# Attention of a decoder layer in float32: values' parts in one operand, scores over half the rows, keys projected before part of the queries, WO's high parts on two engines

## The chip, the cores and the metric

One core of one Trainium2 chip runs the kernel. The metric is the device time of one execution in microseconds (us); lower is better. Engines are named as in the profile: PE is TensorE (its weight loads PEld), DVE is VectorE, ACT is ScalarE, POOL is GpSimd, SP starts the DMAs.

## The reference

One layer over 1024 rows of width 1024, all in float32. The part that the change touches is the token mixer, sliding-window attention with 16 query heads and 4 key/value heads of 64:

```
u   = rmsnorm(x, mix_g)
qkv = u @ wqkv                     # 1024 x 1536
q   = rmsnorm(q heads, gq);  k = rmsnorm(k heads, gk)
s   = q . k / 8 - slope[h] * dist  # per 128-row block, over its own and the previous block
p   = softmax of s within 0 <= dist < 128, with one learned sink per head in the denominator
h   = x + (p @ v) @ wo
```

After it come a squared-ReLU MLP of width 4096 and a gated embedding, which the change leaves alone.

## The kernel before

Products of float32 numbers are made from two parts of each operand: HI, the value rounded to the type float32r, and LO, what is left. A product then takes three passes over TensorE (`PASSES`: HI-HI, HI-LO, LO-HI). For an operand that another engine makes, ACT copies the HI part out of PSUM or a raw buffer and DVE subtracts to make the LO part.

The attention stage walks over 8 blocks of 128 rows (`body(n)`), each in 4 groups (`j`), one group for each key/value head and its 4 query heads. Every engine has its own list of instructions with this order written out by hand, and the engines meet at semaphores; an engine never goes past a wait. In the parts' names, `k` is the projection of keys and values (512 columns), `q0` and `q8` those of query heads 0 to 7 and 8 to 15.

TensorE's list in a block (`body`, L1999): scores of the group (L1947), then what belongs to the group, then `weigh_values` of two groups ago (L1973), then `turn_probs` of the last group (L1963, transposes of the probabilities). Group 0 has the last 6 matmuls of q8 ahead of its scores and `turn_x` (L1891, the next block's x). Group 1 has the next block's q0 projection with `turn_q` of q8 (L1935) between its fifth and sixth k-tile; group 2 has the projection of `k`; group 3 `turn_q` of q0, 18 matmuls of q8 and `turn_k` (L1924).

Scores: q's HI part stands in one half of the 128 rows of `qT` and its LO part in the other, while k stands in both halves of `kT`, as HI and as LO. So a full-row matmul with k's HI and one with k's LO give all four products of a head: 8 matmuls of 256 columns a group. Values: `vz` keeps each head's values between zeros, so that a matmul of 128 weight columns and 256 moving columns puts two heads of a pair on the upper or the lower 64 output rows: 3 passes, 2 sides and 2 halves of keys make 12 matmuls of 256 columns, all summed in one bank. ACT copies that bank out in one instruction (`attention_out`, L949).

DVE in a group: `add_bias` (L1366) merges the two halves of keys with two predicated copies (L1374), adds the bias and takes the maximum for four heads (L1387) and makes `nmax` (L1392). ACT's `exps` (L931) follow, then DVE's `invert` and `scale_probs` (L1401), PE's `turn_probs`, ACT's `pT_hi_part` (L942), DVE's `pT_lo_part` (L1408), POOL's `mask_probs` (L757).

The heads' normalisation of each part is `part_squares` on ACT (L876), `head_sums` on DVE (L1305), `head_norm` on POOL (L688: the variance L691 and the power L693), `head_scale` on DVE (L1311), `turn_q` or `turn_k` on PE, and then HI on ACT (L914, L923) and LO on DVE (L1333, L1340). All three parts put their squares into the one buffer `kn`, so each waits for the one before it.

The last block (`last_part`, L961 and L1413) has no next block to project. In its place TensorE starts the projection by WO for row blocks 0 and 1 (`project_out`, L2033), for which ACT makes WO's eight HI units (`wo_hi_unit`, L857) and DVE the eight LO units (`wo_lo_unit`, L1489). SP and its DMAs are the same in both kernels.

## Time and profile before

| what | value |
|---|---|
| median of 3 runs | 1109.57 us (1107.19 to 1109.82) |
| the profiled execution's own time | 1107.26 us |
| its span, first to last instruction | 1105.5 us |
| PE busy | 98% of the span |
| DVE, ACT, POOL busy | 66%, 39%, 13% |
| granted PE clock | 1.0 of 2.4 GHz |

Busy time is summed over an engine's instructions. Consecutive matmuls overlap in the profile, since each is drawn with its way through the array; the pace of a stretch is read from the chain of waits, which gives the pieces one after another. The chain is followed back from the last instruction: at each step to what released it, or to the instruction before it on its engine. In a timeline the number in brackets is the engine's idle time before the instruction, and what ended it.

### The profile page before, as it was taken

To read this page: it belongs to the slowest core of one execution; us is meant where nothing else is said; L and a number is where in the kernel's file an instruction comes from. 1 tells how busy PE (TensorE), PEld (TensorE's weight loads), DVE (VectorE), ACT (ScalarE), POOL (GpSimd) and SP (SyncE) were. 2 spreads that over 40 slices of the span, in tenths; PEclk is the share of its full clock that TensorE was granted. 3 is DMA by queue.
4 is the path that set the end of the run, shared out by engine and by line. 5 is a ranking of instruction groups with operands and counts; after the bars stand their busy time and mean duration, and the time that the engine had idled before them with its cause. 6 is when DMAs were issued, how large, how long until landed. Compare 5 with 4: busy or idle time off the path is not lost.

```text
span 1105.5 us, 14894 instructions
## 1 busy us (share of the span) xinstructions
PE 1084.9 (98%) x5272; PEld 910.3 (82%) x5272; DVE 732.2 (66%) x1130; ACT 429.8 (39%) x776; POOL 148.4 (13%) x272
## 2 busy tenths in 40 slices
PE   7899999998999999999999999999999999999998
PEld 5788888887888888888888888888888888888886
DVE  6677777778454599776667667598777862664222
ACT  7455655566322234323232244453333331333100
POOL 6554444444100000000000000000000000110000
PEclk9999999999999999999999999999999999999999
DMA  7000000040242325254434056998988862112211
GB/s 267 20 20 20 19 19 0 38 184 26 92 138 76 114 73 209 118 191 153 153 132 190 39 191 218 390 411 293 299 285 289 288 227 76 39 39 59 95 39 39
DMA packets 61361, 153.88 MB, mean 139 GB/s; under 512 B 4720, under 2 KB 5752, under 8 KB 61304
## 3 DMA queue, kind: packets, MB, share of 16 engines
q1 hardware_dynamic: 61280, 153.12, 39.0%
q8 instruction: 35, 0.57, 0.2%
q14 instruction: 22, 0.18, 0.1%
q10 hardware_dynamic: 24, 0.01, 0.0%
HBM read 119.03 MB, written 34.08 MB: 138 GB/s over the span
## 4 chain that ended last, share of the span: by engine, by line
PE 90%; DVE 5%; issue 2%; ACT 1%; POOL 1%; ACTq 0%; DVEq 0%; POOLq 0%
PE pair L2204 24%; PE pair L2184 21%; PE pair L1919 10%; PE pair L2056 8%; PE pair L2247 8%; PE pair L2224 4%; PE pair L1990 4%; PE pair L2142 3%; PE pair L1958 2%; PE pair L2260 2%; PE pair L2112 1%; PE pair L1969 1%; PE pair L1943 1%; PE pair L1901 0%; DVE RES L1722 0%
## 5 line engine op out<-in xcount | busy, mean ns | idle before, releaser
L2204 PE MATMUL pair<-uT 128*128 128x512 f32 x1176 | 266.7, 389 | 0.0
L2204 PEld LDWEIGHTS pair<-uT 128*128 128x128 f32 x1176 | 220.7, 188 | 45.8
L1193 ACT ACTIVATE uT<-wo_raw 128x1024 fp32r<-128x1024 f32 x63 | 64.4, 1054 | 104.9 <-PE pair L2204 90.4
L1919 PE MATMUL pair<-WA,xT 128*128 128x512 f32 x384 | 95.9, 398 | 5.3 <-DVE WA L1292 3.8
L1735 DVE TENSOR_TENSOR uT<-wo_raw,uT 128x1024 fp32r<-128x1024 f32 x63 | 74.9, 1221 | 38.8 <-ACT uT L1193 38.7
L675 POOL TENSOR_SCALAR row_var<-row_ssq 128x1 f32<-128x1 f32 x16 | 3.0, 191 | 700.3 <-ACT hn L1092 700.3
L2056 PE MATMUL pair<-WA,oT 128*128 128x512 f32 x384 | 90.3, 392 | 2.6 <-DVE WA L1491 2.1
L1919 PEld LDWEIGHTS pair<-WA,xT 128*128 128x128 f32 x384 | 69.6, 188 | 22.4 <-issue 6.8
L2056 PEld LDWEIGHTS pair<-WA,oT 128*128 128x128 f32 x384 | 71.2, 188 | 17.5 <-issue 3.1
L2184 PE MATMUL pair<-WA,WB 128*128 128x512 f32 x336 | 78.2, 389 | 0.4 <-ACT xr L1168 0.4
L2184 PEld LDWEIGHTS pair<-WA,WB 128*128 128x128 f32 x336 | 63.0, 188 | 13.8 <-DVE WB L1669 0.8
L938 ACT ACTIVATE probs<-probs,nmax 128x129 f32<-128x129 f32 x128 | 50.0, 393 | 42.8 <-DVE nmax L1392 42.6
L2184 PE MATMUL pair<-uT,WB 128*128 128x512 f32 x240 | 56.1, 389 | 0.0
L2184 PEld LDWEIGHTS pair<-uT,WB 128*128 128x128 f32 x240 | 45.0, 188 | 9.6 <-issue 0.3
L1990 PE MATMUL pair<-pT,vz 128*128 128x256 f32 x384 | 52.1, 285 | 0.5 <-DVE pT L1410 0.5
L1990 PEld LDWEIGHTS pair<-pT,vz 128*128 128x128 f32 x384 | 49.1, 190 | 2.1 <-DVE pT L1410 0.7
L1867 DVE TENSOR_TENSOR act_buf<-pair,act_buf 128x512 f32<-128x512 f32 x16 | 11.0, 690 | 55.3 <-PE pair L2260 55.3
L1919 PE MATMUL pair<-WB,xT 128*128 128x512 f32 x192 | 45.3, 391 | 1.7 <-DVE WB L1292 1.7
L1826 DVE TENSOR_TENSOR RES<-RES,pair 128x512 f32<-128x512 f32 x48 | 30.8, 682 | 22.2 <-PE pair L2204 22.2
L2224 PE MATMUL pair<-WA 128*128 128x512 f32 x192 | 45.4, 393 | 0.0
L2247 PE MATMUL pair<-WB,uT 128*128 128x512 f32 x192 | 45.2, 391 | 0.0
L2247 PE MATMUL pair<-WA,uT 128*128 128x512 f32 x192 | 44.8, 389 | 0.0
(203 smaller groups left out, 1876.1 us busy)
## 6 DMA issues: line engine op xcount, KB each, us to landing
wo_raw<-in_m_w SPq DMA_DIRECT2D x53, 512.0 KB, 6.3
wo_raw<-hid_kept SPq DMA_DIRECT2D x36, 512.0 KB, 4.6
hid_kept<-RES SPq DMA_DIRECT2D x28, 512.0 KB, 2.6
emb<-in_m_w SPq DMA_DIRECT2D x20, 512.0 KB, 6.2
RES<-in_m_w SPq DMA_DIRECT2D x8, 1024.0 KB, 6.9
uT_f<-in_m_w SPq DMA_DIRECT2D x6, 1024.0 KB, 6.5
act_buf<-hid_kept SPq DMA_DIRECT2D x11, 512.0 KB, 4.4
hn<-in_m_w SPq DMA_DIRECT2D x11, 512.0 KB, 5.7
```

The lines of the kernel that those rows point to most:

```text
L938: ex = nc.scalar.activation(row, row, ACT.Exp, bias=nmax[:, i, r:r + 1], accum_out=denom[:, i, r:r + 1])
L1193: nc.scalar.activation(operand(t, which, HI), unit(t, which), ACT.Copy).then_inc(op_hi, 1)
L1735: nc.vector.tensor_tensor(operand(t, which, LO), unit(t, which), operand(t, which, HI).bitcast(F32), ALU.subtract).then_inc(op_ready, 1)
L1826: nc.vector.tensor_tensor(RES[:, b, cols], RES[:, b, cols], bank[:], op).then_inc(posted, 1)
L1919: mm = nc.tensor.matmul(proj_bank[X][:], xT[:, s, kt, :], w[:, m, kt, at:at + BANK], start=(kt == 0 and i == 0), stop=(kt == KT - 1 and i ...
L1990: mm = nc.tensor.matmul(pv_bank[:, 0:2 * P], vz[:, kt, s, at:at + 2 * HD], pT[:, m, kt, odd * 2 * P:(odd + 1) * 2 * P], start=(done == 0), ...
L2056: mm = nc.tensor.matmul(out_bank(b, odd, c)[:], oT[:, hf, s, k % 4 * P:(k % 4 + 1) * P], wo_s[:, m, k, c * BANK:(c + 1) * BANK], start=(k ...
L2142: mm = nc.tensor.matmul(ps[i % 4][:], w1_s[:, s, kt, m * P:(m + 1) * P], uT[:, r, kt, th * BANK:(th + 1) * BANK], start=(kt == 0 and q == ...
L2184: mm = nc.tensor.matmul(chain[:, m, :], a_slot[q % 4][:, s, k, m * P:(m + 1) * P], right(i)(r)[:, k, :], start=(opens and k == 0 and n == ...
L2204: mm = nc.tensor.matmul(ps[4 * (j % 2) + m][:], operand(t, 0, s)[:, k, m * P:(m + 1) * P], operand(t, 1, r)[:, k, :], start=(g == 0 and k ...
L2224: mm = nc.tensor.matmul(ps[4 + a % 4][:], hid[:, s, k, b * P:(b + 1) * P], w2_s[:, r, k, c * BANK:(c + 1) * BANK], start=(k == 0 and q == ...
L2247: mm = nc.tensor.matmul(ps[4 + s % 2][:], uT[:, u, kt, b * P:(b + 1) * P], w[:, m, kt, :], start=(kt == 0 and q == 0), stop=(kt == KT - 1 ...
```

## The change

- **Values.** `vz` holds HI and LO of a head side by side as one operand of 128 weight columns. Four matmuls of 512 columns a group give both parts' products: HI values on output rows 0 to 63, LO values on 64 to 127. ACT copies the bank out in four pieces of 64 rows and 256 columns, and DVE adds the LO half in `add_lows`, three groups later in its list. The LO-LO product, left out before, is in. TensorE waits with `pv_copied` for the bank; the rest waits with `attended`.
- **Scores.** `qT` holds two heads on its two halves of rows, HI and LO as separate tiles. Three passes, each over 64 rows, make 12 matmuls of 256 columns a group; neighbouring ones use opposite halves of the rows and different banks. Both gains of the norms are put on the keys. The two predicated copies become one of 512 columns (`merge_scores`).
- **Order.** Each part has its own buffer for squares. TensorE projects three k-tiles of `k` in group 1, the other five and q0's last three in group 2, and turns q0 at the end of group 3 behind `turn_k`. The heads' sums, norms and scales move in ACT's, DVE's and POOL's lists accordingly; on ACT `pT_hi_part` now stands ahead of `attention_out`.
- **WO.** HI units 4 to 7 are made by POOL, 0 to 3 by ACT, and in the last block DVE's LO units stand at other places.

```diff
 Q8_HEAD, Q8_TAIL = range(0, 6), range(6, 8)
+Q0_HEAD, Q0_TAIL = range(0, 5), range(5, 8)
+K_HEAD, K_TAIL = range(0, 3), range(3, 8)
...
+vz = sb("vz", [P, 2, KV, 2, HD], F32R, in_a)
+low_out = sb("low_out", [P, 2, 2 * P], F32, in_a)
...
 pT = sb("pT", [P, 2, 2, BANK], F32R, in_a)
 probs = sb("probs", [P, 2, G, P + 2], F32, in_a)
...
+score_keys = pair[1][:].rearrange("p b (h a n) -> p (b h) a n", h=2, a=2)
 pT_bank = (ps[4], ps[5])
...
+    def wo_hi_unit(k):
+        pool.wait_ge(projected["q8"], NB)
+        pool.wait_ge(wb_in[k], 16)
+        copy(wo_s[:, HI, k, :], wo_raw[:, k, :]).then_inc(wo_hi_pool, 1)
     def place_sinks(n, j):
...
@@ -779,19 +783,25 @@
             x_norm(n + 1)
         place_sinks(n, 2)
         dv_hi_part(n)
-        if not last:
-            head_norm("q0", n + 1)
         mask_probs(4 * n)
-        if not last:
+        if last:
+            wo_hi_unit(4)
+        else:
             keep_v(n)
         place_sinks(n, 3)
         if not last:
             head_norm("k", n + 1)
         mask_probs(4 * n + 1)
-        if not last:
+        if last:
+            wo_hi_unit(5)
+        else:
             shift_k(n + 1)
             place_sinks(n + 1, 0)
+            head_norm("q0", n + 1)
         mask_probs(4 * n + 2)
+        if last:
+            wo_hi_unit(6)
+            wo_hi_unit(7)
     pool.wait_ge(consts_in, 16)
     place_sinks(0, 0)
...
         if j == 3:
+            head_norm("q0", 1)
             mask_probs(2)
     place_sinks(1, 0)
...
+        wait(act, turned[X], b)
         cols = NH[X] * HD
-        nc.scalar.activation(kn[:, 0:cols], proj_bank[X][:, 0:cols], ACT.Square).then_inc(squared[X], 1)
+        nc.scalar.activation(heads[X][:, 0:cols], proj_bank[X][:, 0:cols], ACT.Square).then_inc(squared[X], 1)
...
-    def q_hi_part(X, b, odd):
+                             ACT.Copy, scale=g_both[:]).then_inc(T_hi["k"], 1)
+    def q_hi_part(X, b):
         act.wait_ge(turned[X], b + 1)
...
-        wait(act, scores_ready, 8 * b + (-4 if X == "q0" else 0))
-        rows = q_rows(odd, HI)
-        nc.scalar.activation(qT[rows, q_heads(X, odd), :], turn_bank[X][rows, :].rearrange("p (a n) -> p a n", a=G),
-                             ACT.Copy, scale=gq_s[rows, :]).then_inc(T_hi[X], 1)
+        wait(act, scores_ready, 4 * b + (-2 if X == "q0" else 0))
+        nc.scalar.activation(qT[:, HI, q_pairs(X), :], turn_bank[X].rearrange("p (a n) -> p a n", a=G),
+                             ACT.Copy).then_inc(T_hi[X], 1)
...
         t, i = 4 * n + j, j % 2
...
         act.wait_ge(w_split, U_W1)
         act.wait_ge(pv_done, t + 1)
+        wait(act, attended, t - 1)
         dst = RES[:].rearrange("p b n -> p (b n)")[:, bass.ds(n * D + j * 2 * P, 2 * P)]
-        nc.scalar.activation(dst, pv_bank[:, 0:2 * P], ACT.Copy).then_inc(attended, 1)
+        nc.scalar.activation(dst[0:HD, :], pv_bank[0:HD, 0:2 * P], ACT.Copy)
+        nc.scalar.activation(low_out[HD:P, j % 2, :], pv_bank[HD:P, 2 * P:4 * P], ACT.Copy)
+        nc.scalar.activation(low_out[0:HD, j % 2, :], pv_bank[HD:P, 0:2 * P], ACT.Copy)
+        nc.scalar.activation(dst[HD:P, :], pv_bank[0:HD, 2 * P:4 * P], ACT.Copy).then_inc(pv_copied, 1)
...
@@ -962,25 +962,18 @@
         t = 4 * n + j
         if j == 0:
             wo_hi_unit(0)
-            wo_hi_unit(1)
-            exps(n, j)
-            attention_out(n - 1, 2)
-            pT_hi_part(t - 1, (j - 1) % 2)
-            q_hi_part("q8", n, 0)
-            q_hi_part("q8", n, 1)
-            wo_hi_unit(2)
+        if j == 1:
+            q_hi_part("q8", n)
+        exps(n, j)
+        if j < 2:
+            wo_hi_unit(j + 1)
+        pT_hi_part(t - 1, (j - 1) % 2)
+        attention_out(*before(n, j, 2))
+        if j == 1:
+            v_hi_part(n)
             wo_hi_unit(3)
-            return
-        attention_out(*before(n, j, 2))
         if j == 2:
             oT_hi_half(1, 0)
-        pT_hi_part(t - 1, (j - 1) % 2)
-        if j == 1:
-            v_hi_part(n)
-        exps(n, j)
-        wo_hi_unit(j + 3)
-        if j == 3:
-            wo_hi_unit(7)
...
@@ -991,27 +984,25 @@
                 if not last:
                     xT_hi_half(n + 1, 0)
                     xT_hi_half(n + 1, 1)
-            if j == 3 and not last:
-                q_hi_part("q0", n + 1, 0)
-                q_hi_part("q0", n + 1, 1)
             if last:
                 last_part(n, j)
                 continue
             if j == 1:
-                q_hi_part("q8", n, 0)
-                q_hi_part("q8", n, 1)
+                q_hi_part("q8", n)
+            if j == 2:
+                part_squares("k", n + 1)
+            if j == 3:
+                part_squares("q0", n + 1)
             exps(n, j)
-            if j == 1 and not last:
-                part_squares("q0", n + 1)
-            if j == 2 and not last:
-                part_squares("k", n + 1)
+            if j == 2:
                 stage_v(n + 1)
-            if j == 3 and not last:
+            if j == 3:
                 k_hi_part(n + 1)
+                q_hi_part("q0", n + 1)
+            if not (first and j < 1):
+                pT_hi_part(t - 1, (j - 1) % 2)
             if not (first and j < 2):
                 attention_out(*before(n, j, 2))
-            if not (first and j < 1):
-                pT_hi_part(t - 1, (j - 1) % 2)
             if j == 1:
                 v_hi_part(n)
             if j == 0 and not last:
...
     body(NB - 2)
     body(NB - 1, last=True)
-    attention_out(NB - 1, GROUPS - 2)
     pT_hi_part(NB * GROUPS - 1, 1)
     oT_hi_half(1, 1)
+    attention_out(NB - 1, GROUPS - 2)
     oT_hi_half(2, 0)
     attention_out(NB - 1, GROUPS - 1)
...
+    def q_lo_part(X, b):
+        dve.wait_ge(T_hi[X], b + 1)
+        nc.vector.tensor_tensor(qT[:, LO, q_pairs(X), :], turn_bank[X].rearrange("p (a n) -> p a n", a=G),
+                                qT[:, HI, q_pairs(X), :].bitcast(F32), ALU.subtract).then_inc(T_ready[X], 1)
...
+    def add_lows(n, j):
+        dve.wait_ge(pv_copied, 4 * n + (j + 1))
+        dst = RES[:].rearrange("p b n -> p (b n)")[:, bass.ds(n * D + j * 2 * P, 2 * P)]
+        nc.vector.tensor_tensor(dst, dst, low_out[:, j % 2, :], ALU.add).then_inc(attended, 1)
...
         nc.vector.tensor_tensor(vprev[:], vprev[:], vnext[:], ALU.subtract).then_inc(v_diffed, 1)
     def v_lo_part(b):
-        def values(slot, s):
-            return vz[:, slot, s, HD:(2 * KV + 1) * HD].rearrange("p (v a d) -> p v a d", v=KV, a=2)[:, :, 0, :]
         dve.wait_ge(v_hi, b + 1)
-        nc.vector.tensor_tensor(values(1, LO), vnext[:].rearrange("p (v d) -> p v d", v=KV),
-                                values(1, HI).bitcast(F32), ALU.subtract).then_inc(v_ready, 1)
...
+    def merge_scores(n, j, first):
+        t = 4 * n + j
...
-            stand(dve, scores_ready, 2 * t + (1 + half_bank))
-            nc.vector.copy_predicated(score_keys[half_bank][:, :, 0, :],
-                                      current[:].bitcast(U32).unsqueeze(1).to_broadcast([P, 2, P]),
-                                      score_keys[half_bank][:, :, 1, :]).then_inc(wrapped, 1)
+        stand(dve, scores_ready, t + 1)
+        nc.vector.copy_predicated(score_keys[:, :, 0, :],
+                                  current[:].bitcast(U32).unsqueeze(1).to_broadcast([P, G, P]),
+                                  score_keys[:, :, 1, :]).then_inc(wrapped, 1)
...
-            if r % 2 == 0:
-                stand(dve, wrapped, 2 * t + (1 + r // 2))
+                stand(dve, wrapped, t + 1)
             nc.vector.tensor_tensor_reduce(
-                probs[:, i, r, 0:P], score_keys[r // 2][:, r % 2, 0, :],
+                probs[:, i, r, 0:P], score_keys[:, pos(r), 0, :],
                 bias[:, G * j + r, :], 1.0, 0.0, ALU.add, ALU.max, rmax[:, i, r:r + 1]).then_inc(biased, 1)
...
     def last_part(n, j):
         t = 4 * n + j
+        merge_scores(n, j, False)
+        add_lows(*before(n, j, 3))
+        add_bias(n, j, False)
         if j == 0:
             head_sums("q8", n)
-            add_bias(n, j, False)
-            wo_lo_unit(0)
+        wo_lo_unit((0, 2, 4, 5)[j])
+        invert(n, j)
+        scale_probs(n, j)
+        if j == 0:
             head_scale("q8", n)
+        if j == 1:
+            q_lo_part("q8", n)
+        pT_lo_part(t - 1, (j - 1) % 2)
+        if j == 0:
+            v_diff(n)
             wo_lo_unit(1)
-            pT_lo_part(t - 1, (j - 1) % 2)
-            v_diff(n)
         if j == 1:
-            q_lo_part("q8", n, 0)
-            q_lo_part("q8", n, 1)
-            add_bias(n, j, False)
-            pT_lo_part(t - 1, (j - 1) % 2)
             v_lo_part(n)
-            wo_lo_unit(2)
             wo_lo_unit(3)
         if j == 2:
-            add_bias(n, j, False)
             oT_lo_half(1, 0)
-            pT_lo_part(t - 1, (j - 1) % 2)
-            wo_lo_unit(4)
-        if j == 3:
-            add_bias(n, j, False)
-            pT_lo_part(t - 1, (j - 1) % 2)
-            wo_lo_unit(5)
-        invert(n, j)
-        scale_probs(n, j)
         if j == 3:
             wo_lo_unit(6)
             wo_lo_unit(7)
...
+            merge_scores(n, j, first)
+            if not (first and j < 3):
+                add_lows(*before(n, j, 3))
             add_bias(n, j, first)
             if j == 0:
-                if not last:
-                    xT_lo_half(n + 1, 0)
-                    xT_lo_half(n + 1, 1)
-                head_scale("q8", n)
+                xT_lo_half(n + 1, 0)
+                xT_lo_half(n + 1, 1)
+                head_sums("q8", n)
             if j == 1:
-                q_lo_part("q8", n, 0)
-                q_lo_part("q8", n, 1)
+                q_lo_part("q8", n)
+                v_diff(n)
             if j == 2:
                 if isinstance(n, int) and n == NB - 2:
                     oT_lo_half(0, 0)
                     oT_lo_half(0, 1)
-                if not last:
-                    head_sums("k", n + 1)
-                    head_scale("q0", n + 1)
-                    head_scale("k", n + 1)
-            if j == 3 and not last:
-                q_lo_part("q0", n + 1, 0)
-                q_lo_part("q0", n + 1, 1)
+                head_sums("k", n + 1)
+            if j == 3:
+                head_sums("q0", n + 1)
             invert(n, j)
-            if j == 1 and not last:
-                head_sums("q0", n + 1)
+            if j == 2:
+                head_scale("k", n + 1)
             scale_probs(n, j)
-            if j == 3 and not last:
+            if j == 3:
+                head_scale("q0", n + 1)
                 k_lo_part(n + 1)
+                q_lo_part("q0", n + 1)
             if not (first and j < 1):
                 pT_lo_part(t - 1, (j - 1) % 2)
             if j == 0:
-                v_diff(n)
+                head_scale("q8", n)
             if j == 1:
                 v_lo_part(n)
     flat = RES[:].rearrange("p b n -> p (b n)")
     def wo_lo_unit(k):
-        dve.wait_ge(wo_hi, k + 1)
+        if k < 4:
+            dve.wait_ge(wo_hi, k + 1)
+        else:
...
     nc.vector.tensor_scalar(columns[:, KT:KT + 2], ps[5][:, 0:2], 1.0, None, ALU.mult).then_inc(mix_ready, 1)
     dve.wait_ge(mix_ready, 2)
-    nc.vector.tensor_scalar(gq_s[:], gq_col, HD ** -0.5, None, ALU.mult).then_inc(mix_ready, 1)
+    nc.vector.scalar_tensor_tensor(out=g_both[:], in0=gq_col, scalar=HD ** -0.5, in1=gk_col, op0=ALU.mult,
+                                   op1=ALU.mult).then_inc(mix_ready, 1)
     lo_unit(1, "kv", 1)
...
     oT_lo_half(1, 1)
+    add_lows(NB - 1, 1)
+    add_lows(NB - 1, 2)
...
     add_attention(0, False)
+    add_lows(NB - 1, 3)
...
...
         wait(pe, biased, 4 * t)
-        for r in range(G):
-            dst = score_bank[r // 2][:, (r % 2) * 2 * P:(r % 2 + 1) * 2 * P]
-            for m in (HI, LO):
-                mm = nc.tensor.matmul(dst, qT[:, G * j + r, :], kT[:, m, j, :, :].rearrange("p a n -> p (a n)"),
-                                      start=(m == HI), stop=(m == LO))
-            if r % 2 == 1:
-                mm.then_inc(scores_ready, 1)
+        for a in range(2):
+            for i, (s, m) in enumerate(PASSES):
+                for odd in range(2):
+                    rows = slice(odd * HD, (odd + 1) * HD)
+                    mm = nc.tensor.matmul(score_bank[odd][:, a * 2 * P:(a + 1) * 2 * P],
+                                          qT[rows, s, G // 2 * j + a, :],
+                                          kT[rows, m, j, :, :].rearrange("p a n -> p (a n)"),
+                                          start=(i == 0), stop=(i == 2))
+        mm.then_inc(scores_ready, 1)
...
         for kt in (1, 0):
             if kt == 0:
                 pe.wait_ge(pT_masked, 2 * t + 2)
                 pe.wait_ge(v_ready, 2 * n + 2)
-            for s, m in PASSES:
-                for odd in range(2):
-                    at = 2 * HD * j + (0 if odd else HD)
-                    mm = nc.tensor.matmul(pv_bank[:, 0:2 * P], vz[:, kt, s, at:at + 2 * HD],
-                                          pT[:, m, kt, odd * 2 * P:(odd + 1) * 2 * P],
-                                          start=(done == 0), stop=(done == 11))
-                    done += 1
+            for m in (HI, LO):
+                mm = nc.tensor.matmul(pv_bank[:], vz[:, kt, j, :, :].rearrange("p s d -> p (s d)"),
+                                      pT[:, m, kt, :], start=(done == 0), stop=(done == 3))
+                done += 1
         mm.then_inc(pv_done, 1)
...
+                    project("q0", n + 1, kts=Q0_HEAD)
                 turn_q("q8", n, after_x=not last)
                 if not last:
-                    project("q0", n + 1, kts=range(5, KT))
-            if j == 2:
-                if not last:
-                    project("k", n + 1)
+                    project("k", n + 1, kts=K_HEAD)
+            if j == 2 and not last:
+                project("k", n + 1, kts=K_TAIL)
+                project("q0", n + 1, kts=Q0_TAIL)
             if j == 3 and not last:
-                turn_q("q0", n + 1)
                 project("q8", n + 1, kts=range(KT) if isinstance(n, int) and n == NB - 2 else Q8_HEAD)
                 turn_k(n + 1)
+                turn_q("q0", n + 1)
             if last and j == 1:
                 project_out(0, False, ks=range(0, 2))
             if last and j == 2:
...
```

## Rows read from the trace of the kernel before

**Rows 1.** The page: busy time by engine, and the chain that ended last by engine.

```profile
PE 1084.9 (98%) x5272; PEld 910.3 (82%) x5272; DVE 732.2 (66%) x1130; ACT 429.8 (39%) x776; POOL 148.4 (13%) x272
...
PE 90%; DVE 5%; issue 2%; ACT 1%; POOL 1%; ACTq 0%; DVEq 0%; POOLq 0%
```

**Rows 2.** Windows by block: first of 31.5, a middle one, the last; us, then each engine.

```profile
33.20:64.67 31.47, 27.98 (x162) 23.96 (x163) 22.13 (x71) 16.51 (x51) 16.12 (x35) 1.00 0.06 18
155.44:185.71 30.27, 30.21 (x191) 26.92 (x190) 22.35 (x72) 17.71 (x54) 13.88 (x25) 1.00 0.06 17
...
246.10:283.86 37.76, 32.94 (x201) 28.58 (x200) 29.39 (x76) 23.40 (x60) 14.99 (x18) 1.00 0.13 48
```

**Rows 3.** Chain through the middle block at 155.44: start us, us, what.

```profile
155.44 0.95 PE pair L1958 x8
156.40 0.87 PE pair L1901 x8
157.27 1.43 PE pair L1990 x12
...
160.09 3.43 PE pair L1919 x15
...
177.65 4.37 PE pair L1919 x18
```

**Rows 4.** Groups by form, 64.67 to 246.1: busy us, mean ns, idle before.

```profile
L1958 PE MATMUL pair<-kT,qT 128*128 128x256 f32 x194 | 28.7, 290 | 0.0
...
L928 ACT ACTIVATE qT<-pair,gq_s 64x512 fp32r<-64x512 f32 x24 | 16.4, 683 | 18.0 <-PE pair L1943 17.7
...
L920 ACT ACTIVATE kT<-pair,columns 128x512 fp32r<-128x512 f32 x6 | 4.1, 690 | 1.8 <-PE pair L1932 1.5
```

**Rows 5.** Timeline of ACT in the middle block: start us, us, what.

```profile
158.53 0.41 ACT L938 ACTIVATE probs<-probs,nmax 128x129 f32<-128x129 f32 x1 [0.57 <-DVE nmax L1392]
...
160.09 0.36 ACT L955 ACTIVATE RES<-pair 128x256 f32 x1
160.36 0.58 ACT L947 ACTIVATE pT<-pair 128x512 fp32r<-128x512 f32 x1
```

**Rows 6.** Timeline of DVE in the middle block.

```profile
156.11 0.69 DVE L1308 TENSOR_REDUCE q_ssq<-kn 128x8 f32<-128x512 f32 x1 [0.70 <-ACT kn L891]
156.71 0.75 DVE L1374 COPY_PREDICATED pair<-current,pair 128x256 f32<-128x256 uint32 x2
...
158.44 1.29 DVE L1301 TENSOR_TENSOR xT<-pair,xT 128x512 fp32r<-128x512 f32 x2
159.65 0.68 DVE L1321 TENSOR_TENSOR qn<-pair,q_rstd 128x512 f32<-128x512 f32 x1
...
161.66 0.41 DVE L1354 TENSOR_TENSOR vprev<-vprev,vnext 128x256 f32<-128x256 f32 x1
```

**Rows 7.** Timeline of POOL in the middle block.

```profile
157.37 1.65 POOL L693 TENSOR_TENSOR q_rstd<-q_var,half 128x8 f32<-128x8 f32 x1
...
179.68 1.05 POOL L737 TENSOR_SCALAR kT<-kT 128x1024 fp32r<-128x1024 f32 x1
```

**Rows 8.** Timeline of PE in the last block.

```profile
251.53 0.66 PE L1943 MATMUL pair<-ident,qn 128*128 128x128 f32 x4 [0.66 <-DVE qn L1321]
...
257.92 1.19 PE L1958 MATMUL pair<-kT,qT 128*128 128x256 f32 x8 [1.09 <-DVE rmax L1387]
261.17 1.62 PE L2056 MATMUL pair<-WA,oT 128*128 128x512 f32 x6 [2.06 <-DVE WA L1491]
...
267.19 2.96 PE L2056 MATMUL pair<-WA,oT 128*128 128x512 f32 x12 [0.19 <-issue]
```

**Rows 9.** Groups by form in the last block, 246.1 to 284.

```profile
L1491 DVE TENSOR_TENSOR WA<-wo_raw,WA 128x1024 fp32r<-128x1024 f32 x8 | 9.6, 1215 | 0.0
...
L861 ACT ACTIVATE WA<-wo_raw 128x1024 fp32r<-128x1024 f32 x8 | 8.1, 1049 | 0.0
...
L763 POOL TENSOR_SCALAR_AFFINE_SELECT pT<-pT 128x512 fp32r<-128x512 f32 x6 | 5.9, 982 | 1.4 <-DVE pT L1410 1.2
```

109 lines of the change are left out of this document (40 added, 69 removed).

## The prediction

> **What bounds the kernel now.** I read the page first, then the windows by block of rows, the chain of waits through one block, and the timelines of the engines in that block. The profiled execution took 1107.26 us with a span of 1105.5; the median of the three runs is 1109.57, 2.3 above it, so differences are worked out against the profile and put on the median. TensorE is busy for 98% of the span and carries 90% of the chain [rows 1]. The change touches only the attention stage, from about 33 to 284 us. There a middle block takes 30.27 us and TensorE is busy for 30.21 of them, DVE for 22.4, ACT for 17.7, POOL for 13.9 [rows 2]. The chain through such a block is TensorE alone, piece after piece [rows 3]: whatever is taken off TensorE counts, until another engine's answer comes late. The last block is different: 37.76 us with 32.9 busy [rows 2].
>
> **TensorE's own work.** (1) Values: 12 matmuls of 256 columns take 1.43 [rows 3]; four of 512 columns at 3.43/15 = 0.229 take 0.91. That is -0.52 for each of 32 groups, -2.1 a block. (2) Scores: 8 matmuls of 256 columns take 0.95, 0.119 each. They become 12, each over 64 of the 128 rows, issued in pairs on opposite halves and into different banks. No row shows a half-row matmul. Lower bound: both of a pair run together, 6 x 0.119 = 0.71; upper bound: each takes its own turn, 12 x 0.119 = 1.43; a gain below 0.71 is excluded, since 6 x 256 columns still pass. I take 0.71, the nearest row being that same 256-column matmul, since the two of a pair read other partitions and write other banks. That is -0.24 a group, -0.96 a block. (3) The same 72 projections and 36 transposes (8 in 0.87, so 4 in 0.44). The 18 projections at 177.65 take 4.37 [rows 3] instead of 18 x 0.229 = 4.1: the refill after a short wait for the keys' normalisation; that wait goes, for the keys are now ready earlier. So TensorE's work in a block falls from 30.27 to 30.27 - 2.1 - 0.96 - 0.3 = 26.9.
>
> On (2) the Trainium skill (TensorEngine Tiling (Array Packing), Key Properties) says that tiles on different rows can load and multiply in parallel, and also that changing the tiling mode drains TensorE. By the first sentence the sum is the one above; what the second would make of it is a rival below.
>
> **The other engines' work.** Each group gets three more ACT copies: 0.27 to 0.28 from one start to the next for 256 columns (160.09 to 160.36 [rows 5]), +3.4 a block; half the partitions save nothing (64x512 takes 0.68, 128x512 0.69 [rows 4]). The queries' high part becomes one copy of about 0.6 for two of 0.68, -1.6 a block. DVE gets add_lows, like the 128x256 subtraction at 161.66: 0.41 long [rows 6], of which 0.08 lies in the next one's start as with the other lines, so 0.33; +1.3 a block. It loses the second half of the queries' low part and the scalar operand, about -1.6. POOL's copies in the loop are the same, only later in its order. All of that costs nothing by itself, hidden beside TensorE by engines with 8 us or more to spare; it costs where it stands in a chain that TensorE waits for. Two such chains follow.
>
> **Stall A, turn_q of q8.** The squares of q8 are now summed after the two xT lows, not before the scores are merged. From the end of scores(n,0): 0.1 hand-over; from the first copy of the merge to the step after nmax 1.73 (156.71 to 158.44), 0.06 less for one copy of 512 columns instead of two, 0.33 more for the lows: 2.0; xT lows 1.21 (to 159.65); sums 0.69 [rows 6]; then POOL, from the sums' end at 156.80 to the end of q_rstd at 159.02: 2.22 [rows 6, 7]; head_scale 0.68 and 0.07 of hand-overs: 6.95. TensorE meanwhile has 0.87 + 0.91 + 0.44 + 0.71 + 3.43 = 6.36. It waits 0.6, and refills for 0.2 (a turn_q that had waited took 0.66 at 251.53, a fed one takes 0.44 [rows 3, 8]). Queued behind it are the first keys' projection, a value product and turn_probs(0); they start later by as much, and what they need has long landed, so nothing is added.
>
> **Stall B, turn_q of q0.** Keys are projected first, so q0's sums come in group 3, not in group 1. From the end of turn_probs(1): pT's high copy on ACT 0.66, its low on DVE 0.60 (the low one stands before the next merge in DVE's order), merge to nmax 2.0, sums 0.69, POOL 2.22, head_scale 0.68, hand-overs 0.07: 6.9. TensorE has scores 0.71, 18 projections 4.10 and turn_k 0.44: 5.25. It waits 1.7 and refills 0.2. A block then takes 26.9 + 0.8 + 1.9 = 29.6, a gain of 0.65 for 3.1 us of work removed and a wait of 0.3. Blocks 1 to 5: -3.2. Block 6 keeps all 24 q8 matmuls in group 3 (1.37 more cover), pays 0.4 for the two oT lows placed before the keys' sums: stall B 0.4, gain about 1.4. Block 0 (31.47 with 27.98 busy [rows 2]) has the same chain B with more in it: scores(0,3) start at 18.1, DVE's bias is done at 21.3, POOL makes four bias tiles (1.4) before it normalises q0 (2.2), head_scale and turn_q end at 26.4, a value product, turn_probs and six projections (2.7) follow: 29.1, gain 2.3. Up to the last block: -6.9.
>
> **The last block**, counted from the start of its scores (before: 246.10). WO's high parts 4 to 7 go to POOL (1.05 for the like copy of 1024 columns; more beside DVE's subtractions, the affine_select with 0.98 on the mean is slowed here [rows 7, 9]), and four of ACT's eight copies of 1.05 [rows 9] go. I cost these at nothing: each is asked for some us after POOL can make it, except the last two, which come some 2 us before TensorE's turn. What it costs if that cover is gone is the +7 below. On it: turn_q of q8 at 7.0 (before 5.4) by chain A with the pT low of group 2 ahead of it. Then DVE's order puts WO's low part 2 before scale and q8's low part, and that unit waits for ACT's exps(1) and then high part 2: head_scale ends at 6.9, pT low, v_diff and WO low 1 at 8.9, merge to nmax(1) at 11.0, exps 1.6 (158.53 to 160.09 [rows 5]) and 0.1 for the last, high 1.05, low 1.2 [rows 9], reciprocal and scale 0.8, q low 0.6, so scores(2) start at 16.3; they started at 11.8 [rows 8]. Part of it was lost before as well: the projection stood until 15.1 for the same WO part [rows 8]. oT's low half of row block 1 now comes late too: the values' lows and WO low 3 end at 19.1, nmax(2) at 21.1, exps(2) 22.8, pT high 23.3, four output copies 24.4, oT high 25.0, low 25.7, against 21.1 [rows 8]. From there TensorE has 12 + 12 + 24 projections, two value products, two transposes: 13.9, to 39.6. Then the last value product needs its bank, read by attention_out(30), which ACT holds behind oT's high half, and that waits for this very projection: 0.1 + 0.6 + 4 x 0.28 = 1.8, and 1.1 for the product with refill: 42.5 where the kernel before stands at 37.76 [rows 2]. +4.7. **Sum:** -6.9 + 4.7 = -2.2, so 1107.5 on the median: no difference that a measurement of this kernel can tell (0.3% is 3.3 us). The last term's own bounds are +1 (if DVE's and ACT's units come as early as before) and +7 (POOL's copies late by their contention).
>
> **Rivals.**
> *The halves don't run together.* Scores cost 1.31 (two loads one after another: 8 transposes, whose 128 columns leave only the load to set the pace, take 0.109 each [rows 3]) to 1.43. Per block +2.4 to +2.9, of which stall A gives back 0.6 to 0.8 and B 0.5: +1.3 to +1.6 against the forecast, 7 blocks, +9 to +11 and some 0.5 in the last: 1117 to 1119. It decides once a group of scores costs over about 1.1. For it: no row shows sharing. Against: the operands lie on separate rows and banks. The Trainium skill (TensorE: Matmul & The Clock Gate, LDWEIGHTS) has a load cost by columns, whatever the rows, which allows this case if loads of two halves queue. Chance 0.26; slower.
> *A drain at each change between full and half rows.* A matmul of 256 columns is 290 ns long at a pace of 119 [rows 4], so 0.17 is in the pipe; to empty it twice a group makes scores 1.05: +1.3 a block, -0.6 of stalls, about +5 in all: 1112. This is what the skill's rule on drains would give. Chance 0.14; same or slower.
> *The two stalls are smaller than worked out* (DVE finishes its earlier steps sooner, or a hand-over hides): half of them gone is -9, none left and the last block unharmed is -3.3 x 7 + 1 = -22, 1087. For it: TensorE was never waiting on those engines before. Against: each link is a row. Chance 0.17; faster.
> *The last block is not harmed* though the others go as forecast: -6: 1103.5. Chance 0.08.
>
> **Numbers.** Forecast 0.35 as it stands; around it, errors of 0.3 a block either way are +-2. Faster by over 0.3%: 0.17 + 0.08 + 0.06 of the forecast's. Within: the forecast's 0.25, 0.07 of the drain. Slower: 0.26, 0.07 and 0.04 of the forecast's. The range leaves out the far end of the small stalls and half of the no-sharing case's tail: 1098 to 1120.5.
>
> **What would show it.** Values: four 128x512 matmuls in 0.91 a group. Scores: 0.71, 1.05 or over 1.3 from first to last. Stall A: TensorE waits some 0.6 for qn before turn_q of q8; stall B: some 1.7 for qn in front of turn_q of q0, a block of 29.6. Last block: scores(2) at 16.3 from its start, and the last value product late behind ACT. The forecast is wrong if blocks fall to 28 or below (the chains are shorter), or rise over 30.3 (the halves don't share).

## The result, and the profile after

The changed kernel takes 1124.65 us (median of 6 runs, 1123.69 to 1125.87) against 1109.69 of the kernel before beside it: ratio 1.0141, 95% interval 1.0126 to 1.0155. Slower, and outside the range of the prediction. Its profiled execution took 1123.71 with a span of 1122.0, 16.5 longer than before. The page, to be held against [rows 1]:

```profile
PE 1079.5 (96%) x5144; PEld 884.5 (79%) x5144; DVE 732.8 (65%) x1114; ACT 451.8 (40%) x852; POOL 156.8 (14%) x275
...
PE 79%; DVE 10%; POOL 4%; issue 3%; ACT 2%; DVEq 0%; ACTq 0%; POOLq 0%
```

TensorE is busy for 5.4 us less, and its share of the chain fell from 90% to 79%: DVE and POOL have joined it. The windows by block, as in [rows 2] (a middle block, block 6, the last one; length, busy PE, PEld, DVE, ACT, POOL, granted clock, DMA share, GB/s):

```profile
157.70:188.91 31.21, 28.97 (x174) 23.14 (x174) 22.15 (x70) 21.03 (x65) 14.66 (x25) 1.00 0.05 17
220.12:250.43 30.31, 28.96 (x173) 23.17 (x172) 22.65 (x71) 20.77 (x64) 13.80 (x24) 1.00 0.40 154
250.43:299.97 49.54, 35.29 (x169) 27.59 (x170) 34.20 (x78) 25.56 (x72) 19.28 (x22) 0.87 0.07 24
```

A middle block takes 0.94 more than before (31.21 against 30.27), although TensorE is busy for 1.24 less; ACT has 3.3 more to do. The three windows don't all begin at the same point of a block, so the sum goes by TensorE's timelines, from the first scores of one block to those of the next. The scores of block 1 start at 63.81 instead of 64.51, so 0.7 is gained up to there. Blocks 1 to 5 take 4.9 more together, block 6 takes 0.35 more (30.38 for 30.03), and the last block 11.3 more (49.34 for 38.02): -0.7 + 4.9 + 0.35 + 11.3 = 15.9 of the 16.5. The last block's granted clock is 0.87 of 2.4 GHz on the mean, where it was 1.00. TensorE's timeline of the middle block:

```profile
160.38 0.60 PE L1964 MATMUL pair<-ident,probs 128*128 128x128 f32 x4
160.91 0.98 PE L1952 MATMUL pair<-kT,qT 64*128 64x256 f32 x12
162.12 3.72 PE L1911 MATMUL pair<-WA,xT 128*128 128x512 f32 x15 [0.23 <-DVE xT L1291]
166.19 0.66 PE L1935 MATMUL pair<-ident,qn 128*128 128x128 f32 x4 [0.36 <-DVE qn L1311]
...
176.67 1.07 PE L1984 MATMUL pair<-pT,vz 128*128 128x512 f32 x4
177.58 0.60 PE L1964 MATMUL pair<-ident,probs 128*128 128x128 f32 x4
178.11 0.98 PE L1952 MATMUL pair<-kT,qT 64*128 64x256 f32 x12
179.02 4.38 PE L1911 MATMUL pair<-WA,xT 128*128 128x512 f32 x18
183.24 0.60 PE L1924 MATMUL pair<-ident,kn 128*128 128x128 f32 x4
185.50 0.66 PE L1935 MATMUL pair<-ident,qn 128*128 128x128 f32 x4 [1.66 <-DVE qn L1311]
```

The same three pieces of the kernel before, for the step from the transposes to the scores:

```profile
175.60 0.60 PE L1969 MATMUL pair<-ident,probs 128*128 128x128 f32 x4
175.95 1.20 PE L1958 MATMUL pair<-kT,qT 128*128 128x256 f32 x8
176.99 0.60 PE L1943 MATMUL pair<-ident,qn 128*128 128x128 f32 x4
```

Read from start to start: a value product takes 0.91 (176.67 to 177.58; 1.43 in [rows 3]). A group of scores takes 0.91 (178.11 to 179.02) where it took 1.04, but the four transposes ahead of it take 0.53 where they took 0.35, so the two together went from 1.39 to 1.44. In group 0, behind projections, the last six projections and the scores went from 2.43 to 2.48. The waits are those of stalls A (0.36) and B (1.66, from 183.24 to 185.50 instead of 0.36), and one for xT.

The last block, TensorE's timeline and then windows of stretches behind its waits:

```profile
258.86 0.66 PE L1935 MATMUL pair<-ident,qn 128*128 128x128 f32 x4 [3.77 <-DVE qn L1311]
259.27 4.71 PE L2048 MATMUL pair<-WA,oT 128*128 128x512 f32 x12
...
268.88 0.98 PE L1952 MATMUL pair<-kT,qT 64*128 64x256 f32 x12 [3.54 <-DVE qT L1332]
...
280.07 4.58 PE L2048 MATMUL pair<-WA,oT 128*128 128x512 f32 x12 [3.42 <-issue]
...
297.93 2.04 PE L1984 MATMUL pair<-pT,vz 128*128 128x512 f32 x4 [2.33 <-ACT RES L955]
```

```profile
258.80:264.50 5.70, 5.64 (x19) 4.25 (x20) 4.44 (x15) 1.79 (x8) 1.93 (x3) 0.70 0.00 0
...
268.80:276.00 7.20, 7.12 (x36) 5.65 (x38) 6.78 (x17) 1.93 (x9) 3.08 (x3) 0.76 0.01 2
...
280.00:285.50 5.50, 5.43 (x17) 4.28 (x18) 3.92 (x14) 1.66 (x8) 0.00 (x0) 0.69 0.27 95
```

TensorE waits four times for 2.3 to 3.8 us, where the kernel before waited for 2.06 at most [rows 8]. Behind each of these four waits it runs for a while at the lower of its two levels: the 12 projections at 280.07 take 4.42 to the next start; at full clock they take 2.84. The length of a wait alone does not tell whether that happens. In block 0 the changed kernel waits 2.38 for qn, at 60.46, and the granted clock behind it stays at 1.00.

### The profile page after: what moved, and what is told of

It reads as the page before. It is cut to its first block, busy times and chain, and to the rows that moved or that the text cites. A ratio compares the mean times of both kernels' runs of the same rounds, so it can differ in the third digit from the quotient of the medians.

```text
span 1122.0 us, 14671 instructions
## 1 busy us (share of the span) xinstructions
PE 1079.5 (96%) x5144; PEld 884.5 (79%) x5144; DVE 732.8 (65%) x1114; ACT 451.8 (40%) x852; POOL 156.8 (14%) x275
## 4 chain that ended last, share of the span: by engine, by line
PE 79%; DVE 10%; POOL 4%; issue 3%; ACT 2%; DVEq 0%; ACTq 0%; POOLq 0%
PE pair L2196 24%; PE pair L2176 21%; PE pair L2048 8%; PE pair L2239 8%; PE pair L1911 4%; PE pair L2216 4%; PE pair L2134 3%; POOL q_rstd L693 2%; PE pair L2252 2%; PE pair L1984 2%; DVE probs L1381 1%; PE pair L2104 1%; PE pair L1952 1%; DVE pair L1365 1%; DVE qn L1311 1%
## 5 line engine op out<-in xcount | busy, mean ns | idle before, releaser
L2048 PE MATMUL pair<-WA,oT 128*128 128x512 f32 x384 | 95.0, 406 | 3.4 <-issue 3.4
L2048 PEld LDWEIGHTS pair<-WA,oT 128*128 128x128 f32 x384 | 74.5, 197 | 20.0 <-issue 3.6
L932 ACT ACTIVATE probs<-probs,nmax 128x129 f32<-128x129 f32 x128 | 50.2, 395 | 31.2 <-DVE nmax L1386 31.2
L1911 PE MATMUL pair<-WB,xT 128*128 128x512 f32 x192 | 48.0, 399 | 1.4 <-DVE WB L1282 1.4
L1254 ACT ACTIVATE act_buf<-pair 128x512 f32<-128x512 f32 x16 | 9.6, 598 | 89.7 <-PE pair L2239 84.0
L2176 PE MATMUL pair<-WA,slot_ring 128*128 128x512 f32 x192 | 44.8, 389 | 0.0
```

The lines of the kernel that those rows point to most:

```text
L932: ex = nc.scalar.activation(row, row, ACT.Exp, bias=nmax[:, i, r:r + 1], accum_out=denom[:, i, r:r + 1])
L1911: mm = nc.tensor.matmul(proj_bank[X][:], xT[:, s, kt, :], w[:, m, kt, at:at + BANK], start=(kt == 0 and i == 0), stop=(kt == KT - 1 and i ...
L2048: mm = nc.tensor.matmul(out_bank(b, odd, c)[:], oT[:, hf, s, k % 4 * P:(k % 4 + 1) * P], wo_s[:, m, k, c * BANK:(c + 1) * BANK], start=(k ...
L2176: mm = nc.tensor.matmul(chain[:, m, :], a_slot[q % 4][:, s, k, m * P:(m + 1) * P], right(i)(r)[:, k, :], start=(opens and k == 0 and n == ...
```

## The experiments

All ratios are against the kernel before, run beside. "Block" is from one block's scores(0) to the next one's; "last" goes from scores(0) of the last block to the first projection behind the last value product, both from start to start in TensorE's timeline of the profiled execution. Before: 30.3 and 38.0. Where two numbers stand under "block", the blocks alternate between them.

| kernel | median us | ratio (95%) | block | last |
|---|---|---|---|---|
| changed | 1124.65 | 1.0141 (1.0126, 1.0155) | 31.2 | 49.3 |
| last_old | 1119.35 | 1.0077 (1.0061, 1.0094) | 31.2 | 44.2 |
| last_act | 1118.12 | 1.0082 (1.0060, 1.0105) | 31.2 | 42.4 |
| two_copies | 1117.43 | 1.0075 (1.0054, 1.0096) | 31.0 | 45.9 |
| old_order | 1133.13 | 1.0200 (1.0183, 1.0217) | 31.5, 33.1 | 49.4 |
| order_last | 1124.89 | 1.0136 (1.0119, 1.0153) | 31.5, 33.1 | 42.0 |
| values_only | 1127.68 | 1.0171 (1.0138, 1.0204) | 32.1, 33.7 | 41.8 |
| values_late | 1113.51 | 1.0038 (1.0028, 1.0048) | 30.6 | 41.4 |
| values_two_low | 1128.72 | 1.0173 (1.0140, 1.0206) | 31.4 | 52.1 |
| values_late_low | 1128.91 | 1.0171 (1.0140, 1.0202) | 31.4 | 51.0 |
| after_best | 1131.89 | 1.0204 (1.0177, 1.0230) | 31.9 | 52.3 |
| after_late | 1123.64 | 1.0120 (1.0100, 1.0140) | 32.0, 33.6 | 41.0 |
| order_tuned | 1111.51 | 1.0017 (1.0006, 1.0027) | 30.4 | 41.9 |
| values_tuned | 1107.60 | 0.9976 (0.9966, 0.9985) | 29.9 | 42.0 |
| **values_mix** | **1103.47** | **0.9946 (0.9934, 0.9958)** | 29.3 | 42.4 |

One execution each: same_half 1126.16 (block 31.2), one_half 1139.62 (block 33.4).

### What half a row costs: same_half, one_half

```diff
# same_half
-for i, (s, m) in enumerate(PASSES):
-    for odd in range(2):
+for odd in range(2):
+    for i, (s, m) in enumerate(PASSES):
# one_half
-rows = slice(odd * HD, (odd + 1) * HD)
+rows = slice(0, HD)
```

> The changed kernel with the scores' matmuls ordered so that three neighbours use the same half of the rows. If opposite halves run together (theory), the pace goes from 76 ns a matmul to 119, so 12 take 1.43 from start to start instead of 0.9, and a middle block grows from 31.2 by 4 x 0.5, less about 0.5 that the waits for qn give back: 32.5 to 33.3. If a half-row matmul is simply faster by itself (rival), the pace stays at 76 ns and the block at 31.2.

> The changed kernel with all twelve score matmuls on partitions 0 to 63, so the odd heads' scores are those of the even ones. If a half-row matmul of 64x256 is short by itself (76 ns from one to the next, against the 118 of a full-row one), the twelve still take 0.89 to 0.91 and the block 31.2. If it is the two halves that run together, the twelve take 1.3 to 1.45 us, the block 31.6 to 33.2, and the total is 1137 to 1150 us.

TensorE's timelines, same_half and then one_half:

```profile
159.21 0.97 PE L1952 MATMUL pair<-kT,qT 64*128 64x256 f32 x12
160.12 1.10 PE L1893 MATMUL pair<-ident,xb 128*128 128x128 f32 x8
```

```profile
187.44 1.69 PE L1952 MATMUL pair<-kT,qT 64*128 64x256 f32 x12
189.05 4.40 PE L1911 MATMUL pair<-WA,xT 128*128 128x512 f32 x18
```

With three neighbours on one half, then three on the other, a group of scores still takes 0.91, as the rival of that run had said: the order of the halves does not matter. With all twelve on one half it takes 1.61 (187.44 to 189.05), more than the 1.3 to 1.45 expected, so the rival (a half-row matmul is short by itself) falls. The block of 33.4 is 2.2 longer for 4 x 0.70 of added scores; the rest is given back at waits.

How the 0.91 come about is seen by counting the scores' matmuls in a window of 0.52 us from the first one on, in the changed kernel and in one_half (line L1952 on PE alone: window, length, busy with the count, granted clock, DMA share, GB/s):

```profile
178.10:178.62 0.52, 0.51 (x8) 1.00 0.00 0
```

```profile
187.42:187.94 0.52, 0.51 (x4) 1.00 0.00 0
```

Read singly, the changed kernel's twelve start in twos, 3 ns apart (178.11, 178.33, 178.45, 178.58, 178.69, 178.81), and one_half's start one by one. From the second start on both go at the same pace: 0.12 from one pair to the next, and 0.12 from one matmul to the next, the pace of a full-row matmul in the kernel before. So the two halves share fully, 59 ns a matmul, and six pairs would take the 0.71 of the lower bound. What is lost lies at the ends of a group. From the last transpose's start to the first score it is 0.20, where the kernel before has 0.03 between them; from the first pair to the second 0.22 (0.20 before); from the last pair to the next piece 0.20 (0.12 before). That is 0.28 lost against 2 x 0.12 saved. In one_half the 0.20 in front and behind are there as well, so they come with the change between full and half rows, and not with the pairing. order_tuned and values_tuned below, alike but for the form of the scores, agree: the four transposes ahead take 0.53 in the one and 0.35 in the other.

### Undoing the last block: last_old, last_act

In last_old ACT's and DVE's lists of the last block are those of the kernel before, while POOL still makes WO's units 4 to 7; in last_act ACT makes all eight, as before.

```diff
# ACT, both, groups 1 to 3; DVE likewise
-exps(n, j)
-if j < 2:
-    wo_hi_unit(j + 1)
-pT_hi_part(t - 1, (j - 1) % 2)
 attention_out(*before(n, j, 2))
...
+pT_hi_part(t - 1, (j - 1) % 2)
...
+exps(n, j)
# last_act
+wo_hi_unit(j + 3)
```

> The changed kernel, with ACT's and DVE's lists of the last block in the order of before (WO's high parts 4 to 7 still on POOL). Theory, the last block's loss is made by WO's low part 2 ahead of q8's low part, oT behind exps and copies, and the last output copy behind oT: scores(2) start near 12 after the block's first scores, not 18.4, no stretch of the last block runs at half clock, and the time falls by 8 to 12 us to 1112 to 1117. Rival, POOL's copies and their contention with DVE cause it: under 3 us are gained and the half-clock stretches stay.

> The changed kernel with the last block's lists of ScalarE, VectorE and GpSimd wholly as before: ScalarE makes all eight WO highs. Between this and the run last_old lies only who makes WO highs 4 to 7. Theory: in last_old the 4.59 us wait for a WO low came from GpSimd's late highs and the contention of its copies; here the last block takes 40.5 to 42 instead of 44.2, total 1115 to 1118. Rival (ScalarE, with its four copies a group, is now the late one): last block 44 to 46, total 1119 to 1123.

TensorE's longest wait in the last block, in the waits of last_old and of last_act (in total, times, longest):

```profile
PE pair L2054 <- DVE WA L1486: 4.6, 1, 4.6
```

```profile
PE pair L2047 <- DVE WA L1479: 3.7, 1, 3.7
```

The new places in ACT's and DVE's lists cost 5.3 us, where 8 to 12 had been expected. The theory holds in part: scores(2) start 13.7 after the block's first scores, for 18.45 in the changed kernel and near 12 in the expectation, and the half clock does not go away, as had been expected, but stands behind the waits that end at 259.20 and 271.34. With WO's units on POOL the last block of the profiled execution is 1.8 longer than in last_act. The times don't show a difference: the medians are 1.2 apart, but each against the kernel before beside it the two are at 1.0077 and 1.0082. Taking those units off ACT gains nothing, and the wait for a WO low grows. 42.4 is still 4.4 above before: that part comes from the value product's copies and additions, as values_only (41.8, WO and order as before) shows.

### The order of blocks: old_order, order_last

The projections, norms and sums of blocks 0 to 6 stand in the order of the kernel before, the new forms of values and scores stay; order_last has last_old's last block too.

```diff
# TensorE; ACT, DVE and POOL accordingly
     turn_q("q8", n, after_x=not last)
     if not last:
-        project("k", n + 1, kts=K_HEAD)
+        project("q0", n + 1, kts=Q0_TAIL)
 if j == 2 and not last:
-    project("k", n + 1, kts=K_TAIL)
-    project("q0", n + 1, kts=Q0_TAIL)
+    project("k", n + 1)
 if j == 3 and not last:
+    turn_q("q0", n + 1)
...
     turn_k(n + 1)
-    turn_q("q0", n + 1)
```

> The changed kernel, with TensorE's projections and the heads' sums, norms and scales of blocks 0 to 6 put back where they stood before (q0 whole in group 1, k in group 2, q0 turned at the start of group 3, q8's sums before the merge). Theory, the waits for qn are made by the new order: TensorE's waits for qn go from 13.3 us to under 2, a middle block is 28.4 to 28.9, and the time is 15 to 18 us below the changed kernel: 1107 to 1110. Rival, the waits come from DVE and ACT having more work (add_lows, four copies): the block stays over 30 and the waits move to turn_probs or the scores.

> Both orders put back, so only the new forms of values and scores and WO's split remain. Theory: the gains add, 1097 to 1101, below the kernel before by 9 to 12 us: 2.05 a block less for the values, 0.5 more for the scores. Rival, one order's gain hides the other's: not below 1105.

Both theories were far off, and both rivals came true (blocks over 30 with the waits elsewhere; not below 1105): the old order is 8.5 slower than the new with the changed last block, 5.5 with the old one. It no longer waits for q0 for long (0.48), but for the keys (1.15), and in every second block it runs at the lower clock behind that. TensorE's timeline and windows of old_order:

```profile
153.70 5.96 PE L1913 MATMUL pair<-WA,xT 128*128 128x512 f32 x18 [1.15 <-DVE kn L1317]
```

```profile
151.00:153.70 2.70, 1.07 (x12) 0.66 (x9) 1.64 (x5) 2.63 (x7) 1.90 (x3) 1.00 0.00 0
153.70:159.70 6.00, 6.00 (x20) 4.74 (x21) 4.81 (x16) 1.66 (x8) 1.98 (x3) 0.72 0.00 0
```

So with these forms the new order is the better one; the forms are what costs. In every second block the 18 projections run at 0.72 of the clock after 2.7 us in which TensorE was busy for 1.07; that is the difference of 31.5 and 33.1. In the blocks between, the same wait of 1.15 stands in front of the same 18, and they run at full clock (186.84 to 191.03).

### The values alone: values_only, values_late

values_only is the kernel before with nothing but the values' part of the change, in ACT's and DVE's old order. In values_late one thing moves on ACT, in every block and likewise in the last one:

```diff
-attention_out(*before(n, j, 2))
...
 pT_hi_part(t - 1, (j - 1) % 2)
 if j == 1:
     v_hi_part(n)
+attention_out(*before(n, j, 2))
```

> The kernel before with the values' part of the change alone: four 128x512 matmuls for a group instead of twelve 128x256 ones, four ScalarE copies of 64x256 and VectorE's addition; scores, order and WO as before. Theory C (the four copies are what turns the saving into waits): TensorE saves 0.52 a group, 2.1 a block, but ScalarE's copies end 1.2 us later in every group, ahead of the probabilities' high copy and the values' high part, so the gain in a block is at most half of it: blocks of 29 to 30.5 against 30.26, last block 38 to 41, total 1100 to 1112. Rival (the copies lie in idle time of ScalarE and it is the scores and the order that cost): blocks of 28.1 to 28.5, total 1090 to 1096. If ScalarE's copies are worse than thought: blocks over 31, total over 1113.

> values_only with one thing moved on ScalarE: in each group the probabilities' high copy, and in group 1 the values' high part, stand ahead of the four 64x256 copies instead of behind them. Theory D (the four copies, 1.55 us in a group, cost nothing as busy time and only make late what is queued behind them on ScalarE): the probabilities' low part no longer waits 0.8 us for its high part and the values' low parts follow at once, so merge, norm of the keys and kn come 1 to 1.5 us earlier; blocks of 29 to 30.5 instead of 32.1 to 33.7, total 1105 to 1115. Rival (VectorE's own added work, 0.41 a group for the addition, and the rest of its list are what is late): blocks stay at 31.5 or more, total over 1120.

ACT's timeline of group 1, values_only and then values_late:

```profile
176.71 0.37 ACT L952 ACTIVATE RES<-pair 64x256 f32 x1
177.09 0.38 ACT L953 ACTIVATE low_out<-pair 64x256 f32<-64x256 f32 x1
177.47 0.38 ACT L954 ACTIVATE low_out<-pair 64x256 f32<-64x256 f32 x1
177.87 0.38 ACT L955 ACTIVATE RES<-pair 64x256 f32 x1
178.27 0.60 ACT L943 ACTIVATE pT<-pair 128x512 fp32r<-128x512 f32 x1
178.76 0.41 ACT L907 ACTIVATE vz<-vnext 128x256 fp32r<-128x256 f32 x1
```

```profile
171.56 0.59 ACT L943 ACTIVATE pT<-pair 128x512 fp32r<-128x512 f32 x1
172.04 0.42 ACT L907 ACTIVATE vz<-vnext 128x256 fp32r<-128x256 f32 x1
172.35 0.37 ACT L952 ACTIVATE RES<-pair 64x256 f32 x1
```

The part that takes 2.05 us a block off TensorE makes the kernel 1.7% slower by itself. Theory C had 1100 to 1112, with "blocks over 31, total over 1113" if the copies were worse than thought, and that is what came. The copies start 0.38 to 0.40 apart, not 0.28: 1.56 for four, and everything behind them in ACT's list is late. Putting two copies that DVE waits for ahead of them gives back 14.2 us; the work is the same to the instruction. Theory D holds, with the blocks (30.6) at the slow end of its range.

### Fewer copies: two_copies, values_two_low, values_late_low, after_best, after_late

two_copies reads the bank out in two pieces of 128x256, so high and low parts are not brought together. after_late is last_act with the values' high part ahead of the copies, and in the last block also the high copies of the probabilities. In the three others with "low" or "best" ACT copies the low parts alone and DVE adds them to the high parts in the bank:

```diff
+nc.vector.tensor_tensor(dst[0:HD, :], low_out[0:HD, j % 2, :], pv_bank[0:HD, 0:2 * P], ALU.add)
+nc.vector.tensor_tensor(dst[HD:P, :], low_out[HD:P, j % 2, :], pv_bank[0:HD, 2 * P:4 * P],
+                        ALU.add).then_inc(attended, 1)
```

> The changed kernel with the four 64x256 copies replaced by two of 128x256 (columns 0 to 255 to the result, 256 to 511 to low_out), so high and low parts are not brought together and the values' result is another one. Theory C: two copies take 0.55 to 0.8 instead of 1.6, ScalarE's list runs some 0.9 us ahead in each group, and the waits behind it (xT, the values' low parts, the queries' norm) shrink: blocks of 29.6 to 30.5 instead of 31.21, total 1110 to 1118. Rival (the waits come from the order, in which the norm of the second queries runs late, not from the copies): blocks of 31.0 to 31.2, total 1121 to 1125.

> values_only with two ScalarE copies instead of four: only the low parts (64x256 each) are copied, and VectorE adds each to the high part straight from the bank, two additions of 64x256 instead of one of 128x256. ScalarE saves 0.77 a group, VectorE gains some 0.35. Theory D: what stands behind the copies on ScalarE comes 0.8 earlier: total 1108 to 1118. Rival (VectorE is the late engine): no gain or a loss against values_only, 1125 to 1135.

> Both: two copies, and behind the probabilities' high copy and the values' high part. Theory D: blocks of 28.3 to 30, total 1095 to 1110, and so perhaps below the kernel before. If VectorE is the late one: no better than values_late.

> The changed kernel with the last block's lists as before (ScalarE makes all WO highs, as in last_act), two copies with VectorE's additions from the bank, and the values' high part and probabilities' high copy ahead of the copies. The middle block's longest wait is the norm of the second queries (1.66 us at its transposition), which this does not touch, so its blocks go from 31.2 to 30.6 to 31.0; the last block from 42.4 to 39 to 41; total 1110 to 1115. If blocks fall below 30 the copies were behind that wait too.

> The changed kernel with its own order of projections, the last block's lists as before, and on ScalarE the high parts ahead of the four copies; against after_best only the copies (four and one addition, instead of two and two additions from the bank) differ. If after_best was slow because TensorE waited for VectorE's additions to free the bank (14.7 us of waits there), those waits are gone here: blocks of 31.0 to 31.3, the last block 41 to 42.5, total 1114 to 1118. Rival (the moved high parts are what costs): over 1122.

two_copies gains 7.2, but only 0.2 in a block, so there the rival holds: stall B does not hang on the copies (TensorE still waits 1.42 there); 3.5 are gained in the last block. Its total lies in the range of theory C by luck, since the blocks do not. The real variant with two copies is a loss, since the bank is now free only after DVE's additions: values_two_low came as its rival had said (1125 to 1135). In the blocks it gains on values_only (31.4), in the last block it loses 10. values_late_low had been expected at 1095 to 1110; at 1128.91 it is 15.4 slower than values_late, and 11.6 us of TensorE's waits in its last block are for the additions. TensorE's waits of after_best, up to 300 us:

```profile
PE pair L1982 <- DVE RES L1336: 14.7, 10, 4.5
PE pair L1933 <- DVE qn L1307: 14.3, 12, 2.9
```

Some 11 of the 14.7 lie in the last block, which takes 52; 1110 to 1115 had been expected. after_late was to settle whether the moved high parts or the additions cost. The additions cost 8 us (1131.89 against 1123.64), less than expected. Moving the high parts ahead of the copies costs 5.5 in the changed order as well (last_act 1118.12): its blocks take 0.8 and 2.4 more by turns, its last block 1.4 less. So the rival is right too. Why, DVE's and POOL's timelines show, last_act first, after_late second:

```profile
181.86 0.43 DVE L1338 TENSOR_TENSOR RES<-RES,low_out 128x256 f32 x1 [0.16 <-ACT RES L948]
```

```profile
181.86 1.33 POOL L736 TENSOR_SCALAR kT<-kT 128x1024 fp32r<-128x1024 f32 x1
```

```profile
186.46 1.24 DVE L1338 TENSOR_TENSOR RES<-RES,low_out 128x256 f32 x1 [0.25 <-ACT RES L948]
```

```profile
186.38 1.05 POOL L736 TENSOR_SCALAR kT<-kT 128x1024 fp32r<-128x1024 f32 x1
```

Two instructions meet: the addition of the lows, which stands in front of the maxima and so in stall B, and POOL's shift of the keys. Whichever starts later is drawn out, the addition from 0.43 to 1.24 or the shift from 1.05 to 1.33. The Trainium skill (SBUF — State Buffer, Terms) says that the two engines share a pair of ports and that the loser blocks for the whole instruction; these rows agree. In after_late the addition is drawn out in each of blocks 1 to 5, and the 0.8 lengthens the wait for qn to 2.39 to 2.42. In every second block the clock then falls:

```profile
188.00:193.00 5.00, 2.61 (x16) 2.09 (x15) 3.52 (x12) 2.22 (x9) 1.92 (x2) 1.00 0.00 0
193.00:197.30 4.30, 4.30 (x16) 3.16 (x15) 1.38 (x2) 2.60 (x6) 1.27 (x2) 0.60 0.00 0
```

### DVE's list put right: values_tuned, order_tuned, values_mix

values_tuned is values_late with the queries' sums and the additions of the lows behind the maxima, and the values' lows in group 2. order_tuned is the same with the change's score forms. values_mix moves two additions to where DVE idles and puts the sums first again in the last block. Its additions in groups 1 and 2, against the kernel before:

```diff
 if j == 2:
+    v_lo_part(n)
+    if not first:
+        add_lows(n - 1, 2)
+        add_lows(n - 1, 3)
...
+if j == 1 and not first:
+    add_lows(n - 1, 1)
 invert(n, j)
```

> values_late with VectorE's list put right for the shorter products: the queries' sums and the low additions behind the scores' bias additions instead of ahead of them, the values' low parts behind those of group 2. Theory E (TensorE's saving of 2.05 a block is there and is taken back by waits that VectorE's order makes: in values_late 0.98 before the second scores, 1.18 before the 18 projections that wait for kn, 0.41 for xT): the first two gaps go or fall under 0.3 each, blocks of 28.2 to 29.3 instead of 30.56, total 1097 to 1106, below the kernel before. Rival (VectorE's work as such is the bound, or a further wait stands right behind): blocks of 30 or more, total 1110 to 1114.

> The same lists with the change's score forms (64x256 on half the rows, one copy and one subtraction for a query group, one merge), the order of blocks and the last block as before. Against values_tuned only the scores' forms differ. By the start-to-start times they cost TensorE 0.05 a group (0.2 a block) and spare ScalarE 0.7 and VectorE 0.85 for each of two query groups. If TensorE is the bound by then: 1 to 3 us slower than values_tuned; if VectorE's list is, faster by 2 to 6 us. I expect 0 to 3 slower, total 1098 to 1108.

> values_tuned with two more moves on VectorE: in the blocks the low additions of groups 1 and 2 go where VectorE idles (behind the queries' low parts in group 1, behind the values' low parts in group 2), and in the last block, where no projection gives time, the queries' sums stand ahead of the bias additions again. Theory E: the waits left in values_tuned's blocks (0.61 before the third scores, 0.83 before the 18 projections) lose some 0.4 to 0.5 each, blocks of 28.9 to 29.5 instead of 29.93; in the last block the 3.26 wait for qn and the half clock behind it (12 projections in 4.41 instead of 2.84) go, against 1.6 before the second scores: 1 to 2 us. Total 1100 to 1105. Rival (VectorE's work between the first and third scores is the bound wherever it stands): blocks of 29.8 or more, total 1105 to 1108.

TensorE's timeline at its waits in a block, values_late and then values_mix:

```profile
162.27 1.21 PE L1973 MATMUL pair<-kT,qT 128*128 128x256 f32 x8 [0.73 <-DVE rmax L1393]
...
181.34 4.37 PE L1934 MATMUL pair<-WA,xT 128*128 128x512 f32 x18 [0.93 <-DVE kn L1326]
```

```profile
157.75 0.65 PE L1961 MATMUL pair<-ident,qn 128*128 128x128 f32 x4 [0.38 <-DVE qn L1321]
...
171.56 4.35 PE L1937 MATMUL pair<-WA,xT 128*128 128x512 f32 x18 [0.59 <-DVE kn L1326]
```

By order alone the block falls from 30.56 to 29.93 and 29.30. values_mix is below the kernel before by 0.54%, interval 0.42 to 0.66%: the fastest of all. Its 2.05 saved a block leave 0.97. values_tuned had been expected at 28.2 to 29.3 a block and 1097 to 1106, and came out at 29.9 and 1107.60: theory E holds in its direction only. The wait before the second scores went, the gap before the 18 projections fell from 1.17 to 0.83, and a new one of 0.61 opened before the third scores. values_mix removed the 0.61 and left the 0.83 as it was; its block and its total are as forecast, but the 1 to 2 us expected in the last block did not come (42.4 for 42.0). The score forms cost 3.9 us on top (1111.51 against 1107.60), 0.5 in a block, where 0 to 3 had been expected.

## Why the prediction was wrong

- **Values** (-0.52 a group): right to 0.01; 2.06 a block for 2.1.
- **Scores**, the first step that failed. I took 0.71 for the twelve and put the change between full-row and half-row matmuls at nothing. The pace was as I took it: pairs run together and follow at 0.12. But each group also pays 0.28 where it begins and ends, more than the 0.24 that the shorter row of matmuls saves: -0.96 a block forecast, +0.2 measured. That is 1.2 us a block. Of the rivals, the drain at each change named this place and nearly the size (+1.3 a block) and would have given 1112, and I had given it 0.14; the halves sharing nothing is excluded by the starts in twos and by one_half (1.61 for 0.91). The Trainium skill (TensorEngine Tiling (Array Packing), Key Properties) has both sentences, and both agree with these rows: tiles on different rows overlap, and a change of mode drains. I had weighed only the first.
- **The 18 projections**: 4.22 against 4.20 before from start to start. The 0.3 that I took off was not there: 4.37 is the length to the drawn end of the last one, not the time to the next start.
- **Stalls A and B**: right. 0.36 and a gap of 0.53 in 15 projections for 0.6 + 0.2; 1.66, and 1.90 with the refill, for 1.7 + 0.2. Not foreseen: 0.3 in front of q0 for xT, whose two lows stand behind the addition and, on ACT, behind the four copies. So 29.6 became 31.2: 1.2 for the scores, 0.3 for the projections, 0.3 for xT, less 0.3 on stall A, which leaves 0.1. Blocks 0 and 6, forecast to gain 2.3 and 1.4, gained 0.5 and lost 0.35. Up to the last block the forecast was -6.9 and the measured change +4.3: 11.2 of the 18.7 us between the forecast (-2.2) and the span (+16.5).
- **ACT's copies**: costed at 0.28 each from a 128x256 row, since half the partitions seemed to save nothing; they take 0.39. "It costs where it stands in a chain" was the right question, but I only followed the two chains of the queries' norms, not those of xT, of the values' parts or of the bank.
- **The last block**, the second step that failed: +4.7 forecast, +11.3 measured (49.3 for a forecast of 42.5). The path was as told (scores(2) at 18.45 from the start for 16.3, the projection behind oT's low at 29.6 for 25.7, the last value product behind ACT), each link longer. The first is turn_q of q8, at 8.4 for 7.0: POOL's normalisation takes 3.45 (254.66 to 258.11) for the 2.22 read from a middle block of the kernel before, beside DVE's WO low 0 and its scaling. Then DVE waits for WO's high 2, in front of the scale and of q8's low part:

```profile
265.95 1.23 DVE L1480 TENSOR_TENSOR WA<-wo_raw,WA 128x1024 fp32r<-128x1024 f32 x1 [2.68 <-ACT WA L871]
```

  What I had no term for is the clock: behind these waits TensorE ran at half speed, which lengthens the pieces at 280.07 and 297.93, both on the path, by 1.6 and 0.9. +7 had been named as the bound of the last block's loss; it was passed. The bound came from POOL's copies alone. last_old shows that the new places in the lists cost 5.3 of the 11.3.
- **The sign.** The case "blocks rise over 30.3" that the prediction named happened, but not for its reason: the halves do share.

What stays open: why the change between full and half rows costs these times, and why three neighbours on one half (same_half) also start in twos, for the trace does not say which half a matmul uses. Open too is what decides whether the clock falls behind a wait, and how much of the last block's 3 to 4 us that even the best versions with four-matmul values pay (41 to 42.4 against 38.0) lies in the copies, how much in the additions.

## What to carry to other kernels

When work is taken off the engine that sets the pace, price the instructions that replace it on the other engines by their place in those engines' lists: here the same instructions in another order were worth 24 us (1127.68 to 1103.47), more than the whole saving on TensorE (2.05 a block, 16 in all). Put a copy that only frees a buffer behind the copies that another engine waits for, and an addition that nobody asks for soon where its engine idles. Where a change opens or lengthens waits on TensorE, look for the lower clock behind them: in after_late the wait grows by 0.8 in each block, and the clock takes another 1.6 in every second one. And where a new form of matmul stands in short groups among others, price the step into the group and out of it, not only the pace inside.

## What the runs showed of the hardware that I had not expected

- The next instruction starts 0.38 to 0.40 us after a ScalarE copy of 64x256 out of PSUM in such a row of four, and 0.26 to 0.27 after a copy of 128x256 (two_copies; [rows 5]): a copy of half the partitions is the dearer one.
- Twelve matmuls of 64 rows by 256 columns take 0.91 on two halves, whatever the order of the halves, and 1.61 on one. Inside a group the two halves share fully (0.12 a pair, 0.12 a single matmul on one half); entering and leaving a group costs 0.28, and four transposes ahead lengthen from 0.35 to 0.53.
- A 128x256 addition on VectorE beside a GpSimd copy of 1024 columns takes 1.24 instead of 0.42.
- The granted clock fell to 0.50 to 0.76 of 2.4 GHz in stretches behind waits of 2.3 to 3.8 us (changed kernel, after_late), behind a wait of 2.02 (values_late, at 267.01: 0.52) and already behind 1.2 us of wait after a thin stretch (old_order). It did not fall behind the wait of 2.06 in the kernel before, nor behind 2.38 in block 0 of the changed kernel, while it did behind the same 2.38 in block 0 of two_copies. The length of a wait alone does not decide it.
